# A two-block model on one core: the mixer in a new order, and norm passes and output products that wait tile by tile

## The chip, the cores and the metric

One core of one Trainium2 chip runs the whole program in one launch. The metric is device time in microseconds (us), the median of several executions. In the rows PE is TensorE, DVE VectorE, ACT ScalarE, POOL GpSimd, SP the queue that issues the DMAs.

## The reference, cut to what matters

272 tokens (16 meta tokens and 256) of width 1024, all float32. The first block is a mixer and a PEER layer, the second block two layers of feed-forward, attention, feed-forward. The change lies in the mixer and at the joints of the second block.

```python
u = rmsnorm(h, norm_mix_w)                       # 272 x 1024
z, xbc, dt_raw, conf_in = split(u @ w_in)        # 1024 | 2048 | 16 | 2048
xbc = silu(causal_depthwise_conv(xbc, 4 taps))   # -> xs, bm, cm
dt = softplus(dt_raw + dt_bias)
y = ssd_chunked(xs * dt, ...) + D * xs           # chunked scan over 16 + 128 + 128 tokens
y = groupnorm(y * silu(z)) * norm_w              # y_ssd, 1024 wide
a, g = split(conf_in)
c = causal_depthwise_conv(a * sigmoid(g), 31 taps)
c = silu(layernorm(c) * g + b)                   # y_conf, 1024 wide
h = h + concat(y_ssd, y_conf) @ w_out            # 2048 x 1024
# second block, four times:
h = h + 0.5 * swiglu(rms_norm(h), wi, wo)        # 1024 -> 2 x 2816 -> 1024
```

## The kernel before, in words

Activations lie transposed, features on the 128 partitions in 8 chunks k and tokens on the columns. Weights stream from HBM in units of 128 x 1024 (512 KB) through a ring of four slots. SP (`stream`, L414) reloads a slot once `unit_done` says that the unit before in that slot is used up.

A product of the projections is a *split* product (`split`, L484): ACT copies the unit rounded to fp32r (`part_high`, L388), POOL or DVE subtracts for the remainder (`part_low`, L394), and PE adds three products for each of 8 chunks (L489 to L491): 24 instructions for a unit. The activations are split the same way into `hw_hi` and `hw_lo` (`gain`, L1040). A few products use plain float32 (`whole`, L476; L480), 8 products for a unit, which the trace records as two instructions each.

The order of the work is written out by hand for each engine; engines meet only through counting semaphores, and an instruction that waits holds up all behind it on its engine.

**The mixer before.** The residual h is weighted by the norm's gain and split (L1087 to L1089); the division by the root mean square (`rstd`) is done on every result. PE sums the squares (`stats`, L497), projects dt in plain float32 (L559), and then runs 16 units of `conf`, 16 of `xbc`, 8 of `z` (L654 to L673). DVE goes through 36 events (L1225): it scales a result into SBUF (L1135, L1147 or L1231), does the 4-tap convolution of an xbc unit (L1151, L1153: source SBUF, sum in PSUM), and from event 4 on an eighth-size task of the 31-tap convolution, `conv_taps` (L1114; L1125: 248 taps on 128 x 256, in two alternating sums in PSUM). ACT and DVE run the softplus of dt (L1095 to L1112) before the first event. The scan has eight steps: `decay_rows` on PE, `decay_in` on DVE, `row_exp` on ACT, `decay_out` on DVE, a product with `ecs` on POOL (L2029), `mix_step` on PE, `keep_y` on DVE. Most of them run after the last tap. Then come the layer norm of the conformer half (`mean_mm`, `centred`, `var_mm`), the group norm of the scan half, and, when all 16 chunks of `mix` are ready (L695), the output product: `loop_pair` takes two units for each of 8 output chunks, and DVE adds each to h and splits it (`add_pair`, L1055). SP asks for the `query` weights only after the keys and the spill of h (L435 to L439).

**The joints of the second block.** A feed-forward (`ffn`, L777, L1446, L1863) is 44 units in and 24 units out. PE waits before the out part for all 22 chunks of `gated` (L782). Before the next norm it sums eight chunks of squares, eight plain float32 products (`stats`), and then waits for all eight chunks of `hw`.

Of the kernel before, what the change touches and what calls it, by code (L numbers as in the profile page):

```python
# [14 lines left out]
P = 128  # L15
D = 1024
KD = D // P
# [29 lines left out]
    ("conf", 16, 8, 16, 4), ("xbc", 16, 8, 16, 4), ("z", 8, 8, 8, 4),  # L47
    ("mix_out", 16, 8, 8, 2), ("query", 16, 8, 16, 4),
# [73 lines left out]
def build(nc, a, out):  # L122
    h_spill = nc.dram_tensor("h_spill", (P, KD, SEQ), F32, kind="Internal").ap()
    bias_rows = nc.dram_tensor("bias_rows", (HEADS, P * REL), F32, kind="Internal").ap()
    with ExitStack() as ctx:
# [80 lines left out]
        stat_ready, std_ready, rstd_ready = sem("stat_ready"), sem("std_ready"), sem("rstd_ready")  # L206
        dve_step = sem("dve_step")
# [19 lines left out]

        NORM = {n: i for i, n in enumerate(["mix", "peer", "final", "ffn1", "a", "ffn2", "ffn3", "b", "ffn4"])}
# [5 lines left out]

        with nc.sbuf_tensor("before", [P, GATED_AT], F32):
# [7 lines left out]
        pair_at = m1.at  # L243
        pair_a, pair_g = m1(2, T), m1(2, T)
        state_at = m1.at
        raw = m1(4, SSD_TAPS - 1 + T)
        conv = m1(4, T)
# [5 lines left out]
        hw_mix = m1(KD, T)  # L253
# [6 lines left out]
        b_tok = m1(2, GROUPS * P)  # L260
        ecs, dec_l = m1(2, 512), m1(2, 512)
        m1_end = m1.at
        m1.at = state_at
        state = m1(2, D)
        m1.at = pair_at
        cs_c = m1(2, 512)
        m1.at = pair_at
        gate_std = m1(GROUPS, SEQ)
        gate_rstd = gate_std
        xdtd = Carve(sq[:, :, :].rearrange("p k t -> p (k t)"), KD * T)(2, D)  # L270
        u_rows = big[0:HEADS, P * SEQ - REL:P * SEQ]
        assert m1_end <= P * SEQ - REL
# [57 lines left out]
        sig_ready = sem("sig_ready")  # L330
# [76 lines left out]
        def _(sp):  # L407
# [22 lines left out]
            for s in range(RING):  # L430
                load_unit("conf", s, s)
            stream("conf", 1)
            for name in ("xbc", "z", "mix_out"):
                stream(name)
            sp.wait_ge(hw_ready, 8 * NORM["peer"] + 8)  # L435
# [3 lines left out]
            stream("query")  # L439
# [32 lines left out]
        def _(pe):  # L472
# [11 lines left out]
            def split(units, b, bank_out, hi, lo, m=KD, k0=0, start=True, stop=True):  # L484
# [19 lines left out]

            def bank_wait(name, i, banks):

                o = OUT0[name] + i
                if o >= 4:
                    pe.wait_ge(acc_free, o - banks + 1 if i >= banks else o - 3 if name in ("xbc", "z") else OUT0[name])

            def straight(name, i, parts, n, banks=4):
# [1626 lines left out]
```

## Time and profile before

| | us |
|---|---|
| median of 3 runs (2571.82 to 2574.12) | 2573.2 |
| the profiled execution | 2573.35 |
| its span in the trace | 2571.6 |
| PE busy, share of the span | 2312.1 (90%) |
| DVE busy | 1701.1 (66%) |
| ACT busy | 1245.5 (48%) |
| POOL busy | 189.6 (7%) |

The span runs from the first to the last instruction; the profiled execution's own time is 1.75 us more, and lies 0.15 us above the median. The mixer takes the first 373 us, the rest of the first block lasts until about 1263 us, the second block until the end. Busy shares are averages over stages that have different limits.

### The profile page before, as it was taken

Reading aid. Unit: us, or ns where it says so; the run is one execution under the profiler, and the core shown is the slowest. Engines: PE = TensorE matmul, PEld = TensorE weight load, DVE = VectorE, ACT = ScalarE, POOL = GpSimd, SP = SyncE. Lnnn points to the kernel's source line nnn. Section 1 sums busy time; section 2 is a strip of 40 time slices with the busy share of each in tenths; the row PEclk is TensorE's granted clock in tenths of the full one; section 3 lists DMA queues with packets and bytes.
Section 4 is the critical chain, followed back from the end, with each engine's and each line's share of the span. In section 5 each row is a group of like instructions: output and inputs, shape, how many; then the busy total and the mean of one; then the engine's idle time right before and its main releaser. Section 6 shows DMA issues by size and latency. Waiting matters only on the chain.

```text
span 2571.6 us, 43283 instructions
## 1 busy us (share of the span) xinstructions
PE 2312.1 (90%) x15506; PEld 2110.3 (82%) x15506; DVE 1701.1 (66%) x3103; ACT 1245.5 (48%) x1699; POOL 189.6 (7%) x90
## 2 busy tenths in 40 slices
PE   6848679999997899999699996889999999869999
PEld 6747569999997788888599995569999997647999
DVE  6997427999957755555766557457656754854774
ACT  3323215777776655555466343426546632323653
POOL 4433000000005500000200000000000000000000
PEclk9988889999999999999899997589999999989999
DMA  4321745555552166666455552025565553202555
GB/s 141 123 74 58 115 141 164 185 183 187 184 184 66 38 189 189 189 188 188 139 173 176 169 169 66 0 87 175 163 184 168 171 173 106 66 17 68 186 171 180
DMA packets 107932, 359.35 MB, mean 140 GB/s; under 512 B 12976, under 2 KB 21552, under 8 KB 107728
## 3 DMA queue, kind: packets, MB, share of 16 engines
q1 hardware_dynamic: 105792, 354.04, 43.8%
q10 hardware_dynamic: 2064, 4.33, 1.5%
q8 instruction: 45, 0.74, 0.1%
q14 instruction: 31, 0.25, 0.0%
HBM read 351.90 MB, written 6.42 MB: 139 GB/s over the span
## 4 chain that ended last, share of the span: by engine, by line
PE 78%; DVE 16%; issue 3%; ACT 1%; DMA 1%; SPq 0%; POOL 0%; DVEq 0%; ACTq 0%; POOLq 0%
PE ps L489 17%; PE ps L491 17%; PE ps L490 17%; PE ps L752 14%; PE ps L480 5%; DVE ps L1125 3%; PE ps L502 1%; DVE hot_keys L1387 1%; DVE big L1488 1%; PE ps L981 1%; DVE ps L1153 1%; DVE big L1621 1%; DVE hw_hi L1043 1%; PE ps L920 1%; DVE big L1560 1%
## 5 line engine op out<-in xcount | busy, mean ns | idle before, releaser
L489 PE MATMUL ps<-hw_hi,w_hi 128*128 128x272 f32 (+1 forms) x3104 | 897.0, 289 | 63.4 <-POOL ring_lo L394 25.0
L388 ACT ACTIVATE w_hi<-ring 128x1024 fp32r<-128x1024 f32 x612 | 646.7, 1058 | 523.9 <-DMA ring<-in_ffn_in_dram 148.9
L491 PE MATMUL ps<-hw_hi,ring_lo 128*128 128x272 f32 (+1 forms) x3104 | 893.5, 288 | 0.0
L490 PE MATMUL ps<-hw_lo,w_hi 128*128 128x272 f32 (+1 forms) x3104 | 892.3, 287 | 0.0
L394 DVE TENSOR_TENSOR ring_lo<-ring,w_hi 128x1024 fp32r<-128x1024 f32 x572 | 698.5, 1221 | 215.8 <-ACT w_hi L388 211.5
L489 PEld LDWEIGHTS ps<-hw_hi,w_hi 128*128 128x128 f32 x3104 | 594.6, 192 | 68.9 <-issue 41.0
L491 PEld LDWEIGHTS ps<-hw_hi,ring_lo 128*128 128x128 f32 x3104 | 594.5, 192 | 0.0
L490 PEld LDWEIGHTS ps<-hw_lo,w_hi 128*128 128x128 f32 x3104 | 592.9, 191 | 0.3
L752 PE MATMUL ps<-w_hi,hid_parts 128*128 128x512 f32 x1024 | 280.7, 396 | 2.3 <-DVE hid_parts L1414 2.3
L752 PEld LDWEIGHTS ps<-w_hi,hid_parts 128*128 128x128 f32 x1024 | 193.5, 189 | 47.7 <-issue 2.5
L489 PE MATMUL ps<-gated_hi,w_hi 128*128 128x272 f32 (+1 forms) x704 | 205.2, 291 | 13.2 <-DVE gated_lo L1468 13.2
L491 PE MATMUL ps<-gated_hi,ring_lo 128*128 128x272 f32 (+1 forms) x704 | 204.4, 290 | 0.0
L490 PE MATMUL ps<-gated_lo,w_hi 128*128 128x272 f32 (+1 forms) x704 | 204.1, 290 | 0.0
L1455 DVE TENSOR_TENSOR big<-ps,rstd 128x272 f32<-128x272 f32 (+1 forms) x176 | 77.0, 438 | 135.0 <-PE ps L491 129.5
L752 PE MATMUL ps<-ring_lo,hid_parts 128*128 128x512 f32 x512 | 161.2, 396 | 0.0
L489 PEld LDWEIGHTS ps<-gated_hi,w_hi 128*128 128x128 f32 x704 | 135.9, 193 | 14.0 <-issue 14.0
L480 PE MATMUL ps<-big,ring 128*128 128x256 f32 (+1 forms) x512 | 118.3, 395 | 22.0 <-DVE big L1276 15.8
L490 PEld LDWEIGHTS ps<-gated_lo,w_hi 128*128 128x128 f32 x704 | 136.0, 193 | 0.0
L491 PEld LDWEIGHTS ps<-gated_hi,ring_lo 128*128 128x128 f32 x704 | 135.6, 193 | 0.0
L480 PEld LDWEIGHTS ps<-big,ring 128*128 128x128 f32 x512 | 100.5, 197 | 40.0 <-issue 16.2
L1825 ACT ACTIVATE hid_parts<-big 128x256 fp32r (+1 forms) x128 | 53.4, 418 | 133.4 <-PE ps L752 129.8
L752 PEld LDWEIGHTS ps<-ring_lo,hid_parts 128*128 128x128 f32 x512 | 96.9, 189 | 22.6
(343 smaller groups left out, 2536.0 us busy)
## 6 DMA issues: line engine op xcount, KB each, us to landing
ring<-in_ffn_in_dram SPq DMA_DIRECT2D x176, 512.0 KB, 3.4
ring<-in_down_dram SPq DMA_DIRECT2D x128, 512.0 KB, 3.4
ring<-in_up_dram SPq DMA_DIRECT2D x128, 512.0 KB, 3.4
ring<-in_ffn_out_dram SPq DMA_DIRECT2D x96, 512.0 KB, 3.5
ring<-in_a_in_dram SPq DMA_DIRECT2D x24, 512.0 KB, 3.5
ring<-in_conf_dram SPq DMA_DIRECT2D x16, 512.0 KB, 3.5
ring<-in_xbc_dram SPq DMA_DIRECT2D x16, 512.0 KB, 3.4
ring<-in_mix_out_dram SPq DMA_DIRECT2D x16, 512.0 KB, 3.4
```

Source lines behind the costliest of these rows:

```text
L388: nc.scalar.activation(w_hi[:, u % RING, :], ring[:, u % RING, :], ACT.Copy).then_inc(hi_done, 1)
L394: eng.tensor_tensor(ring_lo[:, u % RING, :], ring[:, u % RING, :], w_hi[:, u % RING, :].bitcast(F32), ALU.subtract).then_inc(split_done, 1)
L480: last = nc.tensor.matmul(bank_out, ring[:, s, k * P:(k + 1) * P], rhs(k0 + k), start=start and k == 0, stop=stop and k == KD - 1)
L489: nc.tensor.matmul(bank_out, w_hi[:, b, w], hi(k0 + k), start=start and k == 0, stop=False)
L490: nc.tensor.matmul(bank_out, w_hi[:, b, w], lo(k0 + k), start=False, stop=False)
L491: last = nc.tensor.matmul(bank_out, ring_lo[:, b, w], hi(k0 + k), start=False, stop=stop and k == m - 1)
L502: last = nc.tensor.matmul(ps[:, 4, c0:T], C(matrix), sq[:, k, c0:T], start=k == 0, stop=k == KD - 1)
L752: last = nc.tensor.matmul(ps[:, 2 * t + half, :], hid_parts[:, part, t * P:(t + 1) * P], weight[:, s, half * 512:(half + 1) * 512], start= ...
L920: last = nc.tensor.matmul(ps[:, (b + 2) % 4, 0:SEQ], ring[:, u % RING, c0:c0 + P], lat[:, k, META:T], start=k == 0, stop=k == 1)
L1125: relay(V_.scalar_tensor_tensor(sums[k % 2], x, V("conf_w", j * CONF_TAPS + k), sums[k % 2], ALU.mult, ALU.add), k == CONF_TAPS - 1)
L1455: V_.tensor_tensor((up_a, up_b)[s % 2][:, p, c0:T], ps[:, s, 0:T - c0], rstd[:, c0:T], ALU.mult).then_inc(acc_free, 1)
L1825: A_(hid_parts[:, c % PARTS, :], at(hid, it * 4 + c), ACT.Copy).then_inc(hid_hi_done, 1)
```

## The change

What it does, stage by stage:

- The mixer's residual is scaled by its norm's gain and by `rstd` first, and then split; results of xbc, conf and z need no scaling. The squares are added in pairs on DVE, so that four products and not eight make the mean. dt is projected as a split product after the second xbc unit.
- The order of units is xbc, conf, z. The 4-tap convolution reads PSUM and sums in SBUF. The softplus of dt lies between the first five xbc events.
- The 31-tap convolution is dealt out: 11 taps after every conf pair (88), 7 in every step of the scan (56), 16 after the gating of y, and the last 88 after the group norm.
- A scan step goes with every z unit. z is copied by ACT, and its silu is done after the last step.
- The output product runs in two halves of the contraction: eight units that need only the scan half, eight that need the conformer half, into the same eight half-banks. `add_halves` adds them to h in the second half.
- SP loads the first four query units ahead of the keys and the spill.
- In the second block, before a, ffn2, ffn3, b and ffn4, POOL adds the eight chunks of squares into one (`sum_squares`), PE makes one product of it, and does so after the first unit of the next stage. That unit waits for `hw` chunk by chunk. ffn1 keeps its old statistics. The out part of every feed-forward waits for `gated` in three portions.
- At the end of a feed-forward's out part DVE splits h before it makes the last unit's remainder; one rounding and one remainder of the next stage are moved ahead of the root and the reciprocal.

```diff
-    ("conf", 16, 8, 16, 4), ("xbc", 16, 8, 16, 4), ("z", 8, 8, 8, 4),
-    ("mix_out", 16, 8, 8, 2), ("query", 16, 8, 16, 4),
+    ("xbc", 16, 8, 0, 4), ("conf", 16, 8, 0, 3), ("z", 8, 8, 0, 3),
+    ("mix_out", 16, 8, 8, 4), ("query", 16, 8, 16, 4),
...
+            for i in range(UNITS["mix_out"]):
+                half, j = i // KD, i % KD
+                u = UNIT0["mix_out"] + i
+                sp.wait_ge(unit_done, u - RING + 1)
+                load_unit("mix_out", 2 * j + half, u % RING)
+            stream("query", 0, 1)
...
                 for k in range(m):
+                    if normed_before is not None:
+                        pe.wait_ge(hw_ready, normed_before + k + 1)
...
+            def summed_stats(norm, c0):
+                pe.wait_ge(sq_sum, (KD - 1) * (SUMMED[norm] + 1))
+                nc.tensor.matmul(ps[:, 4, c0:T], C("mean_d"), sq[:, 0, c0:T], start=True, stop=True).then_inc(stat_ready, 1)
...
+                        if s < 3:
+                            pe.wait_ge(gated_ready, g0 + min(KD * (s + 1), FF_CHUNKS))
...
+            for e in range(16):
+                if e >= 4:
+                    pe.wait_ge(xconv_ready, e - 3)
+                mixed("xbc", e, e % 4, T, normed(0), 0 if e == 0 else None)
+                if e == 1:
+                    project_dt()
+                if e == 9:
+                    turn_dt()
+                if e == 12:
+                    cumulate()
             for e in range(16):
+                if e < 3:
+                    pe.wait_ge(xconv_ready, 13 + e)
+                else:
+                    pe.wait_ge(glu_done, (e - 3) // 2 + 1)
+                mixed("conf", e, e % 3, T, normed(0))
+                if 2 <= e < 5:
+                    turn_chunk(e - 2)
+                if e in (8, 10):
+                    states((e - 8) // 2)
+            decay_rows(0)
             for e in range(KD):
+                if e < 3:
+                    pe.wait_ge(glu_done, (13 + e) // 2 + 1)
+                else:
+                    pe.wait_ge(z_raw, e - 2)
+                mixed("z", e, (16 + e) % 3, SEQ, normed(META))
+                if e < 7:
+                    decay_rows(e + 1)
+                mix_step(e)
...
+            def out_half(half, ready):
+                for j in range(KD):
+                    u = UNIT0["mix_out"] + KD * half + j
+                    pe.wait_ge(slot_loaded[u % RING], (u // RING + 1) * 16)
+                    if half and j >= 4:
+                        pe.wait_ge(acc_free, OUT0["mix_out"] + j - 3)
+                    for k in range(KD):
+                        if j == 0:
+                            pe.wait_ge(ready, k + 1)
+                        last = nc.tensor.matmul(ps[:, (0, 1, 2, 5)[j % 4], (j // 4) * SEQ:(j // 4 + 1) * SEQ],
+                                                ring[:, u % RING, k * P:(k + 1) * P], mix[:, KD * half + k, :],
+                                                start=half == 0 and j < 4 and k == 0, stop=half == 1 and k == KD - 1,
+                                                skip_group_check=True)
+                    last.then_inc(unit_done, 1)
...
+            def xbc_event(i):
+                x, acc = ps[:, i % 4, 0:T], conv[:, i % 4, :]
+                dve.wait_ge(unit_done, UNIT0["xbc"] + i + 1)
+                if i >= 4:
+                    dve.wait_ge(xbc_ready, i - 3)
+                link(V_.tensor_scalar(acc, x, V("ssd_w", i * 4 + 3), V("ssd_b", i), ALU.mult, ALU.add))
+                for k in (2, 1, 0):
+                    late = SSD_TAPS - 1 - k
+                    ins = V_.scalar_tensor_tensor(acc[:, late:T], x[:, 0:T - late], V("ssd_w", i * 4 + k), acc[:, late:T],
+                                                  ALU.mult, ALU.add)
...
+            for i in range(5, 16):
+                xbc_event(i)
+                if i == 10:
+                    copy_dt()
+                if i == 13:
+                    copy_cum()
+            for e in range(16):
+                if e % 2:
+                    gate_pair(e // 2)
+                if 3 <= e < 6:
+                    scale_x(e - 3)
+                if e in (9, 11):
+                    keep_state((e - 9) // 2)
+                if e % 2:
+                    conv_taps(11)
+            for i in range(8):
                 decay_in(i)
+                conv_taps(3)
+                if i >= 1:
+                    keep_y(i - 1)
                 decay_out(i)
+                conv_taps(4)
...
+            def sum_squares(norm, c0):
+                at0 = (KD - 1) * SUMMED[norm]
+                for k in range(1, KD):
+                    pool.wait_ge(sq_ready, 8 * NORM[norm] + k + 1)
+                    if k > 1:
+                        pool.wait_ge(sq_sum, at0 + k - 1)
+                    nc.gpsimd.tensor_tensor(sq[:, 0, c0:T], sq[:, 0, c0:T], sq[:, k, c0:T], ALU.add).then_inc(sq_sum, 1)
```

## Rows read from the trace of the kernel before

**Rows 1.** Stretches of the mixer; busy us of each engine, granted clock, DMA share, GB/s

```profile
40.00:218.00 178.00, 131.81 (x929) 126.19 (x927) 169.00 (x393) 53.05 (x73) 87.73 (x38) 0.88 0.34 107
...
218.00:295.00 77.00, 42.95 (x305) 37.17 (x306) 42.71 (x81) 28.00 (x51) 11.86 (x9) 0.82 0.51 70
...
295.00:354.00 59.00, 58.25 (x256) 50.45 (x256) 9.52 (x23) 0.00 (x0) 0.00 (x0) 0.95 0.42 117
...
354.00:374.00 20.00, 6.63 (x21) 5.47 (x22) 3.04 (x4) 6.23 (x13) 0.00 (x0) 0.57 0.59 210
```

**Rows 2.** Timeline of the start: start us, length us, instruction

```profile
12.51 6.36 PE L502 MATMUL ps<-sq,con 128*128 128x272 f32 x16
...
19.43 1.85 DVE L1037 RECIPROCAL rstd<-std 128x272 f32<-128x272 f32 x1 [2.85 <-ACT std L1702]
...
31.26 0.57 PE L489 MATMUL ps<-hw_hi,w_hi 128*128 128x272 f32 x1 [8.62 <-POOL ring_lo L394]
...
40.29 0.77 DVE L1135 TENSOR_TENSOR big<-ps,rstd 128x272 f32<-128x272 f32 x2
```

**Rows 3.** A stretch in which PE never waits, columns as in rows 1

```profile
1430.00:1480.00 50.00, 50.00 (x402) 50.00 (x401) 29.23 (x37) 21.80 (x25) 0.00 (x0) 1.00 0.62 190
```

**Rows 4.** Timeline of DVE, 106 to 114 us

```profile
106.96 0.44 DVE L1147 TENSOR_TENSOR big<-ps,rstd 128x272 f32<-128x272 f32 x1
...
109.53 0.43 DVE L1142 TENSOR_TENSOR big<-big 128x272 f32<-128x272 f32 x1
...
110.00 3.23 DVE L1125 SCALAR_TENSOR_TENSOR ps<-big,vec,ps 128x256 f32<-128x256 f32 x8
...
113.14 0.44 DVE L1147 TENSOR_TENSOR big<-ps,rstd 128x272 f32<-128x272 f32 x1
```

**Rows 5.** Timeline, 28 to 39 us: POOL beside DVE

```profile
28.68 9.90 POOL L394 TENSOR_TENSOR ring_lo<-ring,w_hi 128x1024 fp32r<-128x1024 f32 x4 [18.16 <-ACT w_hi L388]
...
31.30 2.49 DVE L1105 TENSOR_TENSOR big<-big 16x272 f32<-16x272 f32 x1
```

**Rows 6.** Groups of instructions in the mixer, 0 to 385 us: busy, mean ns, idle before

```profile
L388 ACT ACTIVATE w_hi<-ring 128x1024 fp32r<-128x1024 f32 x46 | 47.8, 1051 | 107.8 <-DMA ring<-in_query_dram 85.5 <-DMA ring<-in_conf_dram 22.3
...
L394 POOL TENSOR_TENSOR ring_lo<-ring,w_hi 128x1024 fp32r<-128x1024 f32 x40 | 95.6, 2397 | 102.0 <-ACT w_hi L388 102.0
```

**Rows 7.** Page, DMA issues: size and us to landing

```profile
ring<-in_xbc_dram SPq DMA_DIRECT2D x16, 512.0 KB, 3.4
```

**Rows 8.** Timeline of DVE in the scan: a step start

```profile
233.79 0.42 DVE L1245 TENSOR_TENSOR big<-ps,rstd 128x256 f32<-128x256 f32 x1 [7.74 <-PE ps L491]
...
248.89 0.69 DVE L1206 TENSOR_TENSOR big<-ps,big 128x512 f32<-128x512 f32 x1 [0.63 <-PE ps L632]
...
251.94 0.69 DVE L1206 TENSOR_TENSOR big<-ps,big 128x512 f32<-128x512 f32 x1 [0.24 <-PE ps L632]
```

**Rows 9.** Timeline of the output product and what follows

```profile
294.80 58.45 PE L480 MATMUL ps<-big,ring 128*128 128x256 f32 x256 [15.76 <-DVE big L1276]
...
373.23 0.47 PE L489 MATMUL ps<-hw_hi,w_hi 128*128 128x256 f32 x1
```

**Rows 10.** Waits of PE after 385 us: total, times, longest

```profile
PE ps L489 <- DVE gated_lo L1468: 13.2, 4, 3.3
```

**Rows 11.** Two stretches just after that wait, columns as in rows 1

```profile
1418.00:1424.00 6.00, 6.00 (x28) 6.00 (x29) 1.92 (x2) 1.06 (x1) 0.00 (x0) 0.52 0.02 4
...
1860.70:1864.00 3.30, 3.24 (x14) 3.25 (x15) 2.09 (x2) 1.06 (x1) 0.00 (x0) 0.50 0.02 5
```

**Rows 12.** Timeline at two norm passes after a residual add

```profile
1486.69 3.83 PE L502 MATMUL ps<-sq,con 128*128 128x272 f32 x16
...
1720.45 3.83 PE L502 MATMUL ps<-sq,con 128*128 128x272 f32 x16
...
1721.95 2.35 DVE L394 TENSOR_TENSOR ring_lo<-ring,w_hi 128x1024 fp32r<-128x1024 f32 x2
...
1723.92 0.49 PE L489 MATMUL ps<-hw_hi,w_hi 128*128 128x272 f32 x1
```

More of the change, by code:

```diff
@@ L226, in chain @@
             return link, relay
+        SUMMED = {n: i for i, n in enumerate(["a", "ffn2", "ffn3", "b", "ffn4"])}
         NORM = {n: i for i, n in enumerate(["mix", "peer", "final", "ffn1", "a", "ffn2", "ffn3", "b", "ffn4"])}
@@ L1075, in add_three @@
                         gain(base, j, c0)
+                    if final and base is not None:
+                        low(name, e + 2)
             def add_single(name, base, c0):
@@ L1268, in _ @@
-            link(V_.reciprocal(rstd[:, 0:SEQ], std[:, 0:SEQ]))
-            for k in range(KD):
-                V_.tensor_tensor(conf[:, k, :], conf[:, k, :], rstd[:, 0:SEQ], ALU.mult).then_inc(ln_in, 1)
+            conv_taps(16)
             for half in range(2):
@@ L1447, in ffn, with group @@
                 g0 = FF_CHUNKS * (f - 1)
-                invert(f"ffn{f}", c0)
                 name = f"ffn{f}_in"
                 u0 = UNIT0[name]
-                with dve.Fori(0, FF_CHUNKS // 2) as it:
+                if f > 1:
+                    low(name, 2)
+                invert(f"ffn{f}", c0)
+                def group(it, first):
                     for s in range(RING):
@@ L1456, in ffn @@
                                          ALU.mult).then_inc(acc_free, 1)
-                        low(name, s + 2, it)
+                        if not (first and s == 0):
+                            low(name, s + 2, it)
                         if s % 2:
@@ L1469, in ffn @@
                                              ALU.subtract).then_inc(gated_ready, 1)
+                if f > 1:
+                    group(0, True)
+                with dve.Fori(1 if f > 1 else 0, FF_CHUNKS // 2) as it:
+                    group(it, False)
                 add_three(f"ffn{f}_out", base, c0)
             ffn(1, 0, VEC["ln_mix"])
+            low("a_in", 2)
             invert("a", 0)
@@ L1734, in _ @@
+            for e in range(4, 18):
+                high("xbc", e)
+                if e >= 7:
+                    xbc_silu(e - 4)
+                if e == 15:
+                    act.wait_ge(cum_mm, 1)
+                    A_(cum[0:META, 0, HEADS:2 * HEADS], ps[0:META, 4, HEADS:2 * HEADS], ACT.Exp).then_inc(cum_exp, 1)
+                    A_(cum[:, 1, HEADS:3 * HEADS], ps[:, 4, 4 * HEADS:6 * HEADS], ACT.Exp).then_inc(cum_exp, 1)
+            xbc_silu(14)
+            xbc_silu(15)
             for e in range(16):
@@ L1872, in ffn @@
                             A_(up_a[:, p, c0:T], up_a[:, p, c0:T], ACT.Silu).then_inc(silu_ready, 1)
+                if f > 1:
+                    group(0, True)
+                with act.Fori(1 if f > 1 else 0, FF_CHUNKS // 2) as it:
+                    group(it, False)
                 name = f"ffn{f}_out"
@@ L2007, in _ @@
             nc.gpsimd.tensor_copy(ident_bf[:, :], ident).then_inc(pads_clear, 1)
[L2009 to L2010 removed]
+            for e in range(UNITS["xbc"] + 10):
+                part_low(nc.gpsimd, "xbc", 0, e)
             for c in range(2):
[L2012 to L2013 removed]
                 n = CHUNKS[c][1]
@@ L2049, in _ @@
             nc.gpsimd.tensor_tensor(bias[:, :, :], bias[:, :, :], bc(mask[:, 0, :], 1, HEADS), ALU.add).then_inc(bias_ready, 1)
+            def sum_squares(norm, c0):
[5 more added lines that the diff above has]
+                    nc.gpsimd.tensor_tensor(sq[:, 0, c0:T], sq[:, 0, c0:T], sq[:, k, c0:T], ALU.add).then_inc(sq_sum, 1)
+            for norm in ("a", "ffn2", "ffn3", "b"):
+                sum_squares(norm, 0)
+            sum_squares("ffn4", META)
 def column_blocks(w):
```

414 lines of the change are left out of this document (196 added, 218 removed).

## The prediction

> **What bounds the kernel now.** I read the page first: PE is busy for nine tenths of the span, but its tenths sag in the first 15%, where DVE shows 9 after 9. Then busy time by stretch, for the mixer alone [rows 1]. From 40 to 218 us DVE works 169.0 of 178 us and PE 131.8: the 31-tap convolution bounds this stretch. From 218 to 295 us nobody is full (PE 42.95, DVE 42.71 of 77): a chain of latencies, in which each engine waits for another. From 295 to 354 us PE works alone on the output product (DVE 9.5 of 59), and from 354 to 374 us PE is busy for 6.6 of 20. Third, the timeline of the start: the first product of a unit comes at 31.26 us and DVE takes the first result at 40.29 us [rows 2]. In the second block PE never waits inside a feed-forward: 402 products in 50 us, 0.124 us each [rows 3], so whatever PE no longer does or waits for there comes off the time one to one, unless something else is late.
>
> **The start.** Four mean products replace eight: 6.36 us for eight at the start [rows 2], so 3.2 us from 12.5 to 15.7 us. The root (1.1 us, an estimate with its table load) and the reciprocal (1.85 [rows 2]) give 18.7 us. New on this path are 8 scalings, 8 roundings on ACT that run beside them, and 8 subtractions. An operation of this kind takes 0.43 us with its wait and about 0.35 without [rows 4], so the first unit could start at 21.8 us. POOL is in the way. While it worked for 9.90 us on four remainders, a DVE operation of 0.43 us took 2.49 us and ended with one of them [rows 5]; I add 1.5 us of that: 23.3 us. The rule behind it is in the Trainium skill, "SBUF — State Buffer", section "Who interferes with whom": DVE with two SBUF inputs and a GpSimd operation that reads SBUF lock each other out. The trace agrees.
>
> The rule speaks against this change, since it puts POOL's remainders beside more such DVE work (scalings, softplus) and adds 35 POOL sums. Events read PSUM and are free of it: L1147 stays at 0.44 us beside POOL [rows 4]. Counting every lock-out gives 301 us for the end of the mixer below, counting none 293.
>
> **xbc.** A unit is 24 products, 3.0 us [rows 3]. The first runs cold, +1.5 us, and ends at 27.9 us. Three more and the dt product, also 24 instructions, end at 40 us. The fifth unit's rounding now stands on ACT behind the softplus and three silus, which wait for DVE's third event; ACT's 1.05 and POOL's 2.4 us for it follow [rows 6]. I put this stall at 6.3 us. Twelve units of 3.0 us, 1.5 us cold and 3 us of small products bring the end to 86.7 us. Does DVE keep up? An event cost 2.57 us, from 106.96 to 109.53 [rows 4], and loses its first instruction, about 0.5. What the trace lacks is a tap from PSUM into SBUF; bounds are 1.7 us for an event (every instruction at 0.43 us) and 2.6 (no gain); I take 2.0, which is 2.57 less that first instruction, since the three accumulating taps stay. Both ends stay under 3.0, so they move the sum by 2 us at most. The weights keep up too: 3.4 [rows 7] + 1.05 + 2.4 us [rows 6] in a ring of four units of 3.0 us.
>
> **conf.** Sixteen units, 48 us; transposes and states about 9 us beside no cover; alternation between PE and DVE 6 us: 149.5 us. DVE's share is less: 88 taps at 0.39 us (3.14 us for eight [rows 4]) make 35 us, with gates, scalings and states 48.
>
> **z and the scan.** Before, a step with no tap in it took 3.05 us and a step with a z unit 11 us, 7.74 of it waiting for PE [rows 8]. In the new step 7 taps (2.75 us), three operations of the scan of 0.69 us [rows 8], their waits and `keep_y` (0.6) make 6.0 us of DVE work. PE needs 2.8 + 1.3 + 1.0 us, inside it. Eight steps: 198 us. The chain of latencies of before now lies under taps.
>
> **To the last tap.** Gating 2.8, 16 taps 6.3, a wait of 2.6 for the statistics, group norm 10 (four reciprocals of 1.8 [rows 2] and eight scalings): 220 us. Then 88 taps, 34.5, and three closings of 1 us: 258 us. The first half of the output product, 8 units of 3.65 (58.45 us for 16 [rows 9]), 29 us, starts at about 212 us and is free, as long as these taps cover it; bare it would cost 29 us.
>
> **The tail.** Mean product 0.5, eight subtractions 2.8, a square and its product 1.2, root 1.8, reciprocal 1.85, first scaling and silu 1: 268 us with the waits. Second half of the product, 29.2 us: 297 us. The query weights are there, so only eight mean products of 0.43 us stand before the first query product: 301 us. Before it came at 373.23 us [rows 9]. **Mixer: -72 us.** The keys and the spill, 1 MB each, now lie beside the loading of query unit 5, which has over 8 us of slack.
>
> **Joints of the feed-forwards.** The wait for the last `gated` is 13.2 us in four [rows 10]. After it PE runs at half clock: granted 0.52 over 6 us, a loss of 2.9 us, and 0.50 over 3.3 us, a loss of 1.65 [rows 11]; the others I take at 1.65. With 8 chunks needed for the first unit and all 22 only 6 us later, both go: -21 us. Before a, ffn3 and b, eight statistics products (3.83 us [rows 12]) become one: -3.0 each, -9, because the first unit's weights and chunks are ready. POOL's last sum (about 0.65 us, from 2.4 for 1024 columns [rows 6]) ends as the first unit does. Before ffn2 and ffn4 the statistics were a cover: product 1 came at 1723.92, and the first remainder of two of 1.2 us from 1721.95 on would allow 1723.15 [rows 12]. This saves 0.8, costs one product of 0.45, and uncovers an idle gap of 2.7 us, after which the clock should fall as it did after 3.3 us: +1.5 each, +3.
>
> **Sum.** -72 - 21 - 9 + 3 = -99 us against the profiled execution's 2573.35: 2474 us. That execution lies 0.15 us above the median of the runs shown, so the median moves alike.
>
> **Rival 1, a larger gain.** DVE is never kept waiting and nothing is locked out. Its work from 28 us on is 16 events (31), softplus and copies (13), 248 taps with closings (106), gates, scalings and states (12), scan (22), norms (13): 197 us, so the last tap falls at 225 instead of 258. That gives 2441 us. For it: DVE had only 9 idle us in 178 before [rows 1]. Against it: xbc now has no taps beside it, and DVE must idle while PE makes 3.0 us units.
>
> **Rival 2, a smaller gain.** The scan steps stay ruled by PE's round trips. If a step costs 9 us instead of 6, because PE falls idle in each and takes its z unit at half clock (5.3 us), the stage is 24 us longer: 2498 us. For it: steps with a z unit took 11 us and PE's mean clock in the scan was 0.82 [rows 1, 8]. Against it: `decay_rows` is now issued a step ahead.
>
> **Rival 3, slower.** One mechanism: the short waits between units, one in nearly each of 40, keep PE at 1.2 GHz through the whole mixer. Each of 40 units costs 2.6 us more (granted 0.52 [rows 11]), 104 us, of which DVE's work could hide some; the eight bare units of the product double, +28. If all of it showed, 2474 + 104 + 28 = 2606 us. It decides from the point where the 99 us are eaten, three quarters of this. Against it: with the waits of before the clock from 40 to 218 us was still 0.88 [rows 1].
>
> **Rival 4, it doesn't do what it says.** The dealt-out taps are a fixed list; if the last 88 ended before the first half of the product did, that half would be bare and the fall 15 to 20 us smaller. Here taps end at 258 and the half at 242, so the margin is 16 us.
>
> **Numbers.** My forecast with its neighbours (2460 to 2488) 0.58; rival 1 0.14; rival 2 0.20; rival 4 0.05; rival 3 0.02; other 0.01. The range leaves out the far half of rival 1 and what lies beyond rival 2: 2450 to 2502. A measurement of this kernel can tell 0.2%, 5 us, from no change; only rival 3 reaches it. Faster 0.97, same 0.01, slower 0.02.
>
> **What would show it.** First unit product near 23 us; a stall of some 6 us before the fifth unit; xbc done near 87, conf near 150, z near 198 us; last tap near 258 us; first query product near 301 us. No wait of PE for the last `gated`, and full clock behind it; one statistics product after the first unit of a, ffn2, ffn3, b, ffn4, and a low clock only in ffn2 and ffn4. I am wrong if the first query product comes outside 285 to 325 us, if more than half of the first output half is waited for, or if the second block shortens by less than 18 or more than 35 us.

## The result, and the profile after

The changed kernel takes 2490.64 us (median of 4 runs, 2487.36 to 2492.97) against 2572.51 of the kernel before in the same runs: ratio 0.9682, 95% interval 0.9665 to 0.9699. The forecast was 2474 us with a range of 2450 to 2502. So the sign and the range held, but 99 us were forecast and 82 came. The profiled execution took 2490.17 us, with a span of 2488.3: 83.2 us less than the one of before.

The page of the changed kernel: busy time, and PE's tenths over the granted clock, in 40 slices of 62 us.

```profile
span 2488.3 us, 42956 instructions
...
PE 2286.5 (92%) x15436; PEld 2086.0 (84%) x15436; DVE 1697.3 (68%) x3067; ACT 1169.0 (47%) x1652; POOL 228.8 (9%) x124
...
PE   6987999999978999999699988799999998778999
...
PEclk8997999999999999999899996599999999989999
```

Busy time by stretch of the mixer, the same view as [rows 1]: conf, the scan, the tail with the first output half, and the second half.

```profile
93.00:152.00 59.00, 54.15 (x402) 51.98 (x401) 45.07 (x103) 19.90 (x26) 39.80 (x18) 0.97 0.42 130
152.00:200.00 48.00, 42.08 (x388) 39.24 (x387) 47.49 (x110) 19.29 (x33) 24.25 (x14) 0.96 0.29 90
200.00:260.00 60.00, 44.02 (x155) 35.10 (x156) 58.06 (x134) 7.59 (x19) 0.00 (x0) 0.77 0.82 145
260.00:302.00 42.00, 37.43 (x165) 32.08 (x164) 18.82 (x43) 14.51 (x29) 0.00 (x0) 0.96 0.35 108
```

Before, nobody was full from 218 to 295 us; now PE is busy for 54 of the 59 us of conf, and DVE for all but 2 us of the scan and of the tail. The timeline of PE and DVE at the places that the prediction named (these rows answer to [rows 2, 8, 9]):

```profile
22.34 0.56 PE L506 MATMUL ps<-hw_hi,w_hi 128*128 128x272 f32 x1 [5.85 <-DVE hw_lo L1156]
...
45.92 0.57 PE L506 MATMUL ps<-hw_hi,w_hi 128*128 128x272 f32 x1 [6.06 <-POOL ring_lo L403]
...
93.91 0.44 DVE L1227 TENSOR_TENSOR big<-ps,big 128x272 f32<-128x272 f32 x1 [4.32 <-ACT big L1819]
...
199.94 0.61 DVE L1290 SCALAR_TENSOR_TENSOR big<-big,vec,ps 128x128 f32<-128x128 f32 x2
...
213.04 2.04 PE L732 MATMUL ps<-big,ring 128*128 128x256 f32 x4 [3.72 <-DVE big L1329]
...
242.05 15.87 PE L732 MATMUL ps<-big,ring 128*128 128x256 f32 x64 [7.65 <-DMA ring<-in_mix_out_dram]
...
261.48 2.74 DVE L1335 TENSOR_TENSOR big<-big,ps 128x256 f32<-128x256 f32 x8 [2.86 <-PE ps L742]
...
302.28 0.47 PE L506 MATMUL ps<-hw_hi,w_hi 128*128 128x256 f32 x1
```

The first query product comes at 302.28 us where it came at 373.23. The second block, at the joint of ffn2 (this answers to [rows 10, 11]; the second line is a stretch behind it), and in front of ffn2's first unit, where the prediction expected its only loss. First all waits of PE for the last eviction at a joint, then the stretch, then timeline and stretch at the norm pass:

```profile
PE ps L506 <- DVE big L1520: 3.6, 4, 0.9
```

```profile
1784.90:1790.00 5.10, 4.98 (x40) 4.98 (x41) 4.19 (x6) 1.97 (x2) 0.00 (x0) 1.00 0.49 124
```

```profile
1643.10 7.82 POOL L2154 TENSOR_TENSOR sq<-sq 128x272 f32<-128x272 f32 x7 [228.03 <-ACT sq L1771]
...
1646.02 0.88 DVE L1097 SCALAR_TENSOR_TENSOR hw_lo<-h,vec,hw_hi 128x272 fp32r<-128x272 f32 x1
1646.82 5.18 DVE L403 TENSOR_TENSOR ring_lo<-ring,w_hi 128x1024 fp32r<-128x1024 f32 x3
...
1648.85 0.57 PE L506 MATMUL ps<-hw_hi,w_hi 128*128 128x272 f32 x1 [3.75 <-DVE ring_lo L403]
...
1653.35 0.62 PE L525 MATMUL ps<-sq,con 128*128 128x272 f32 x2
```

```profile
2286.80:2291.80 5.00, 0.90 (x5) 0.90 (x5) 4.87 (x5) 2.69 (x4) 4.28 (x6) 0.85 0.39 105
2291.80:2296.80 5.00, 5.00 (x25) 4.91 (x24) 2.22 (x2) 0.00 (x0) 1.13 (x1) 0.50 0.00 0
```

At the joint 0.9 us are left of 3.3 and the clock behind it is 1.00. At the norm pass POOL's seven sums stand together, 1.12 us each; beside them DVE's remainders cost 1.73 us each (5.18 for three), and the gain's second part 0.88 instead of 0.50. PE waits 3.75 us, and 4.1 in front of ffn4, where it then runs at a granted 0.50.

### The profile page after: what moved, and what is told of

Read it like the earlier page. It is cut to its first block, busy times and chain, and to the rows that moved or that the text cites. A ratio compares the mean times of both kernels' runs of the same rounds, so it can differ in the third digit from the quotient of the medians.

```text
span 2488.3 us, 42956 instructions
## 1 busy us (share of the span) xinstructions
PE 2286.5 (92%) x15436; PEld 2086.0 (84%) x15436; DVE 1697.3 (68%) x3067; ACT 1169.0 (47%) x1652; POOL 228.8 (9%) x124
## 4 chain that ended last, share of the span: by engine, by line
PE 81%; DVE 13%; issue 2%; DMA 2%; ACT 1%; POOL 0%; DVEq 0%; SPq 0%; ACTq 0%
PE ps L506 18%; PE ps L508 18%; PE ps L507 18%; PE ps L804 14%; PE ps L495 2%; PE ps L732 2%; DVE hot_keys L1449 1%; DVE ps L1214 1%; DVE big L1561 1%; PE ps L1034 1%; DMA ring<-in_mix_out_dram 1%; DVE hw_hi L1096 1%; DVE big L1695 1%; DVE big L1633 1%; PE ps L973 1%
## 5 line engine op out<-in xcount | busy, mean ns | idle before, releaser
L2154 POOL TENSOR_TENSOR sq<-sq 128x272 f32<-128x272 f32 (+1 forms) x35 | 38.8, 1107 | 1047.5 <-ACT sq L1973 587.4
L2133 POOL TENSOR_TENSOR diff<-con,slot_t 128x1024 f32<-128x1024 f32 x32 | 64.6, 2023 | 547.0 <-DVE slot_t L1427 526.4
```

What stands on the lines that cost most here:

```text
L2133: nc.gpsimd.tensor_tensor(diff[:, b, :, :], bc(C("iota"), 1, 8), bc(keys, 2, P), ALU.subtract).then_inc(hot_diff, 1)
L2154: nc.gpsimd.tensor_tensor(sq[:, 0, c0:T], sq[:, 0, c0:T], sq[:, k, c0:T], ALU.add).then_inc(sq_sum, 1)
```

## Where the 83 us come from

I compare the places at which PE stops in both traces. The shift of each such place, and what it grew by since the one before:

| place | before | after | shift | step |
|---|---|---|---|---|
| first query product | 373.2 | 302.3 | -70.9 | mixer -70.9 |
| transposes of the routing | 791.7 | 722.8 | -68.9 | query +2.0 |
| end of ffn1's in units | 1414.6 | 1345.8 | -68.8 | 0 |
| a's head statistics | 1546.3 | 1470.8 | -75.5 | ffn1 joint -4.8, norm a -1.9 |
| end of ffn2's in units | 1857.4 | 1784.1 | -73.3 | norm ffn2 +2.2 |
| end of ffn3's in units | 2065.4 | 1985.8 | -79.6 | ffn2 joint, norm ffn3 -6.3 |
| b's index logits | 2175.1 | 2089.1 | -86.0 | ffn3 joint, norm b -6.4 |
| b's wait for the selection | 2258.1 | 2173.3 | -84.7 | +1.3, no edit in it |
| b's transposes behind the selection | 2279.0 | 2195.4 | -83.6 | +1.2, no edit in it |
| end of ffn4's in units | 2498.8 | 2419.5 | -79.4 | norm ffn4 +4.2 |
| last product | 2566.1 | 2482.8 | -83.3 | ffn4 joint -3.9 |

So the mixer was 1 us off, the query 2 and the second block 13 (-14.4 against -27). The two steps in b are changes of the clock and not of the work (behind the selection it was granted 0.73 over 6 us before and 0.54 after): in the traces of the kernels below, which have b's code unchanged, the first of the two stretches took 81.3 to 84.3 us (83.0 before, 84.3 in the changed kernel) and the second 5.1 to 6.5 (5.1 before, 6.2 in the changed kernel). Likewise ffn4's in part with its norm took 132.6 us in the changed kernel's trace and 131.0 to 131.1 in six of the eight others with the same code there (132.0 and 132.6 in the other two), so up to 1.6 us of its +4.2 are chance.

The experiments go after the terms of the second block first, then after what bounds the new mixer. Of the mixer's 71 us only the hidden half of the output product is tested by taking it out; that the rest comes from the scaled activations, the taps dealt out and the scan beside z is read from the traces and shown by no run.

## The experiments

All are edits of the changed kernel, so their ratios stand against its 0.9682. A ratio's interval is about 0.0015 to either side, 4 us, and a difference of two of them some 5 us; where the effect is smaller, the verdict rests on the stage of the trace that the edit touches.

### POOL's sums: pe_sums_2 and pe_sums_5

```
 def summed_stats(norm, c0):
+    if norm not in SUMMED: return stats(norm, c0)
-SUMMED = {... "a", "ffn2", "ffn3", "b", "ffn4"}
+SUMMED = {... "a", "ffn3", "b"}     (pe_sums_2)
+SUMMED = {}                         (pe_sums_5)
```

> The changed kernel, with the squares of ffn2 and ffn4 no longer summed on POOL: PE does eight statistics products there, still behind unit 0 and with the tile-wise waits kept. Theory (the seven POOL sums of 1.1 us each lock DVE's last gains and lows: lows of 1.7 us where 1.22 would do, gaps of 3.75 and 4.10 us before unit 0 where 2.7 was forecast, and a lower clock after the gap): lows back at 1.22 us, both gaps at 2.4 to 3.0 us, fourteen more products on PE (+1.6 us), together 3 us faster than the changed kernel (1 to 6), 2487.6 us. Rival 1 (the gap is the chain h addition, gain, unit 0 by itself and POOL has no part in it): gaps unchanged, 1.6 us slower. Rival 2 (POOL's sums hide at no cost and the lower clock decides): within 1 us of the changed kernel.

> As pe_sums_2, but the statistics of all five norms go back to eight products on PE behind unit 0. Theory (in front of a, ffn3 and b the squares come one every 9 us, POOL's sums are spread out and lock nothing that is waited for): seven more products at each of the three, 0.8 us each, so 2.4 us slower than pe_sums_2 and about 0.6 us faster than the changed kernel, 2490 us. Rival (POOL's sums cost DVE something there too): no slower than pe_sums_2.

pe_sums_2: ratio 0.9693 [0.9679, 0.9706], 2.8 us slower, which the medians alone can't tell from no change. pe_sums_5: 0.9726 [0.9713, 0.9740], 8.5 us slower again. Both expectations are wrong in the same term. The timeline of pe_sums_2 in front of ffn2, PE and DVE:

```profile
1646.89 0.36 PE L506 MATMUL ps<-hw_hi,w_hi 128*128 128x272 f32 x1 [2.81 <-DVE ring_lo L403]
1651.50 3.83 PE L519 MATMUL ps<-sq,con 128*128 128x272 f32 x16
```

```profile
1645.00 0.50 DVE L1099 SCALAR_TENSOR_TENSOR hw_lo<-h,vec,hw_hi 128x272 fp32r<-128x272 f32 x1
1645.42 3.49 DVE L403 TENSOR_TENSOR ring_lo<-ring,w_hi 128x1024 fp32r<-128x1024 f32 x3
```

Eight statistics products take 3.83 us, one takes 0.62: a norm costs 3.2 us more with eight, not 0.8. I had priced them like unit products of 0.12 us, against the prediction's own [rows 12]. With that, pe_sums_2 adds 6.4 us of products and is 2.8 us longer in the two stages (ffn2 2.38, ffn4 0.45), so POOL's sums cost 3.6 us there; against the 131.0 us that most other traces show for ffn4 it's 2 us. The gap fell from 3.75 and 4.10 to 2.81 and 2.79 and the remainders from 1.73 to 1.16 us each, as the theory had it. pe_sums_5 adds 3 x 3.2 = 9.6 us and is 8.5 longer: in front of a, ffn3 and b the sums on POOL hide nearly whole. So by the trace's stages POOL's sums pay everywhere, and least where they stand close together.

### The joints: joint_whole and joint_free

```
 def loop_3(name, parts, n, g0):
+    pe.wait_ge(gated_ready, g0 + FF_CHUNKS)     (joint_whole)
-    pe.wait_ge(acc_free, o0)                    (joint_free)
...
-            if s < 3:
-                pe.wait_ge(gated_ready, ...)    (joint_whole)
```

> The changed kernel, with the old wait at the joint of the four FFNs: all 22 tiles gated before the first out unit. Theory (of the 17 us that the joints gained 9.6 are the shorter gaps, 0.91 us in place of 3.30, and the rest is the clock that no longer falls behind the gap): gaps back at 3.3 us, a cold stretch behind each, 17 us slower, 2507.6 us (15 to 20). Rival (the clock would stay up, or it fell for another reason): 9.6 us slower, 2500 us.

> The changed kernel, without the wait for the last in unit's eviction in front of the out loop, as the waits on the single banks cover it. Theory (the 0.91 us gap that is left at each joint is that eviction alone): the four gaps go to under 0.2 us, 3 us faster, 2487.6 us (2 to 4). Rival (behind it stands another wait, for the lows of the first out unit or for the last two gated tiles): the gap moves into the third out unit or stays, under 1 us faster.

joint_whole: 0.9742 [0.9729, 0.9755], 15.4 us slower; in the trace the four stages from the last in unit to the last out unit are 18.3 us longer. joint_free: 0.9659 [0.9643, 0.9675], 5.9 us faster. Waits of PE in joint_whole, and the stretches behind its four joints:

```profile
PE ps L506 <- DVE gated_lo L1533: 13.2, 4, 3.3
```

```profile
1352.30:1358.00 5.70, 5.68 (x25) 5.69 (x26) 2.04 (x2) 1.06 (x1) 0.00 (x0) 0.51 0.00 0
1795.70:1801.00 5.30, 5.29 (x23) 5.30 (x24) 2.04 (x2) 1.06 (x1) 0.00 (x0) 0.50 0.02 5
2002.40:2008.00 5.60, 5.56 (x32) 5.57 (x33) 2.07 (x2) 1.06 (x1) 0.00 (x0) 0.70 0.01 3
2436.40:2442.00 5.60, 5.60 (x35) 5.60 (x36) 1.99 (x2) 1.06 (x1) 0.00 (x0) 0.70 0.01 3
```

The 13.2 us of [rows 10] are back to the tenth. Of the 15.4 us (18.3 in the trace), 9.6 are gaps and the other 6 to 9 products at a low clock, granted 0.50 to 0.70: the joint's term is shown, both halves of it. What the prediction missed is the 0.9 us that stays at each joint: the loop's own first line waits until all evictions of the in units are done. joint_free takes that line out, and the trace then has no gap at any joint. The four stages are 4.6 us shorter, 3.6 of it the gaps; what the medians show beyond that is within what two measurements differ by.

### In front of ffn2 and ffn4: ffn_order

```
 ACT:  for k in range(KD):
+          if 5 <= k < 7: high(then, k - 5)
           square(k)
-      high("ffn2_in", 0), high("ffn2_in", 1)   in front of the squares
 DVE:  for j in range(KD):
           add, gain(j)
+          if 5 <= j < 7: low(then, j - 5)
-      first_lows("ffn2_in")                    (ffn4_in alike)
```

> The changed kernel, with ACT's squares of the first five tiles in front of the roundings of the first two ffn2 and ffn4 units, and DVE's low parts of these two units behind the gains of tiles 5 and 6. Theory (unit 0 waits 3.75 and 4.10 us because DVE does the low part behind the last gain, and because POOL's seven sums stand close together and lock it; neither has to be there): gaps under 1 us, POOL's sums one every 3.7 us, the clock stays up behind them, 8 us faster (5 to 11), 2482 us. Rival (the products of unit 1 and the eviction of unit 0 wait for the statistics instead, so most of it comes back as a wait for rstd within the first group): 3 us faster or less.

0.9624 [0.9607, 0.9642], 14.9 us faster by the medians; by the two stages of the trace 4.6 and 6.4, 11 us, of which up to 1.6 us are the chance in the changed kernel's ffn4. The medians' figure holds more chance. PE, POOL and the stretches in front of ffn2 and ffn4:

```profile
1646.97 0.40 PE L506 MATMUL ps<-hw_hi,w_hi 128*128 128x272 f32 x1 [0.53 <-DVE h L1136]
1650.11 0.62 PE L525 MATMUL ps<-sq,con 128*128 128x272 f32 x2
```

```profile
1636.46 1.01 POOL L2152 TENSOR_TENSOR sq<-sq 128x272 f32<-128x272 f32 x1 [2.65 <-ACT sq L1773]
1640.61 1.66 POOL L2152 TENSOR_TENSOR sq<-sq 128x272 f32<-128x272 f32 x1 [3.14 <-ACT sq L1773]
```

```profile
1647.00:1652.00 5.00, 5.00 (x38) 4.92 (x39) 2.76 (x4) 2.55 (x4) 1.02 (x1) 1.00 0.41 112
...
2285.00:2290.00 5.00, 5.00 (x44) 4.97 (x43) 3.12 (x4) 3.68 (x5) 0.00 (x0) 1.00 0.48 130
```

The gap is 0.53 us, the granted clock stays at 1.00 in these stretches, and POOL's sums come one in 3.7 us: 1.01 us with DVE silent, 1.66 beside a DVE remainder. The rival (the wait comes back for the statistics) fell. The loss that the prediction had booked as unavoidable was an order of instructions on ACT and DVE, which the change had left as it was.

### The output product's first half: half_bare_2, spread_z, taps_14_2, spread_taps

half_bare_2 moves the call:

```
-out_half(0, y_norm)
 ... mean product, variance product ...
+out_half(0, y_norm)
 out_half(1, mix_ready)
```

> The changed kernel, with the first half of the output product moved behind the product of the variances, right in front of the second half. Theory (the first half costs 29 us and lies whole beside DVE's last taps, its wait of 7.65 us for a transfer too): it starts where PE now waits for the normed tiles, about 264 us, and ends at 293 instead of the second half's start at 269.7, so 24 us slower, with up to 6 us more for a clock that is low at its start: 2515 us (2511 to 2520). Rival (the first half only displaces waits that would otherwise be there, or DVE's taps ran slower beside it): under 15 us slower.

0.9764 [0.9745, 0.9782], 21.1 us slower (21.4 by the first query product of the trace). The half is hidden, as the theory had it, and DVE's taps ran no faster without it: from PE's sums for the group norm to the end of the last closing it's 55.5 us in both traces. Moved, it cost the low end of what I expected: the two halves run from 265.15 us on as one group of 256 instructions in 55.4 us, without the 7.65 us wait and over what was PE's wait for the normed tiles.

```
-conv_taps(11)
+conv_taps(14)
```

> The changed kernel, with 14 taps of the causal convolution behind each conf pair instead of 11. Theory (DVE idles 14 us of the 59 us of the conf units, and is full from there on, so 24 taps of 0.47 us moved forward leave the tail shorter by what fits the idle time): DVE busy 45 us to 55 us in that stretch, 7 us faster (3 to 11), 2482 us. Rival (PE is busy 54 of these 59 us and waits for the gates: taps in front of a gate push the conf units back by as much as the tail gains): within 1.5 us of the changed kernel.

0.9690 [0.9674, 0.9707], 2.1 us slower, which can't be told from no change: the rival. In the trace the last conf gate comes 3.4 us later (154.55 against 151.16), the scan starts 4.6 us later, and the first output half 4.1 us later. But then DVE finishes its taps early and waits:

```profile
266.22 2.73 DVE L1335 TENSOR_TENSOR big<-big,ps 128x256 f32<-128x256 f32 x8 [12.89 <-PE ps L742]
```

So with the taps moved forward the tail is not bound by taps: PE stands in the first output half until 262.7 us. In the changed kernel this wait is 2.86 us, and half and taps end together (257.9 and 258.6 us). The DMA view of the changed kernel, 195 to 245 us, shows what else holds the half up:

```profile
bias_rows<-big ACTq DMA_DIRECT2D x1, 4224.0 KB, 45.6
ring<-in_mix_out_dram SPq DMA_DIRECT2D x5, 512.0 KB, 15.4
```

ACT issues the bias rows' transfer behind the silus of z, and a weight unit takes 15.4 us beside it (the median of five; the four issued while it ran took 13.2 to 19.2) instead of 3.5.

```
+act.dma_start(bias_rows ...)      in front of the scan's loop
 for e in range(8): high("z", e + 2), row_exp(e), z_copy(e)
-act.dma_start(bias_rows ...)      behind the silus of z
```

> The changed kernel, with the transfer of the relative bias rows (4.2 MB, 45.6 us to landing, begun at 199 us behind the silus of z) issued before the z units, at about 157 us. Theory (this transfer takes the queues while the first output half wants a unit every 3.7 us: the units land in 15.4 instead of 3.5 us, PE waits 7.65 us, and the first half ends at 257.8 us, level with the last taps at 257.7; the z units, one every 5.4 us, can stand the same delay): the 7.65 us wait is gone, the first half ends near 248 us, the taps then set the end alone, DVE's wait for the mean falls from 2.86 to about 1 us, 2 us faster (1 to 3). Rival (the z units' loads come late and stretch the scan): slower.

> As spread_z, with 14 taps behind each conf pair besides, as in taps_14_2. Theory (there DVE ended its taps 12.9 us before the mean was there, since PE was held in the first output half by that transfer): with the transfer out of the way the centring starts at about 254 us instead of 261.5 (changed kernel) and 266.2 (taps_14_2), 7 us faster than the changed kernel (5 to 9), 2483 us. Rival (PE's first half is late because its own start depends on the scan, which comes 5 us later there): under 3 us faster.

spread_z: 0.9743 [0.9726, 0.9760], 15.7 us slower. spread_taps: 0.9703 [0.9686, 0.9721], 5.4 us slower. Half of the theory held: in spread_z PE has no wait for a transfer in the first half any more and DVE waits 1.38 us for the mean, not 2.86. The other half, that z can stand the delay, fell. Timeline of DVE in spread_z:

```profile
174.47 0.69 DVE L1283 TENSOR_TENSOR big<-big,ps 128x512 f32<-128x512 f32 x1 [5.34 <-ACT big L1847]
...
200.42 0.69 DVE L1283 TENSOR_TENSOR big<-big,ps 128x512 f32<-128x512 f32 x1 [7.63 <-ACT big L1847]
```

ACT rounds the next z unit ahead of the row exponentials, so a late transfer (a median of 13.4 us here, by its DMA view) stops ACT, and with it the scan: 5.3 and 7.6 us in two steps. In spread_taps it's 2.5 and 7.7 us. But spread_taps is 10.3 us faster than spread_z (5.2 us by the start of the second half): once no transfer holds the first half up, the taps moved forward do shorten the tail. I had checked only the slack of the ring, not what is queued behind the waiting instruction.

### The start, and the query: highs_first_2, query_load_2

```
+high("xbc", 4)                    (highs_first_2)
 act.wait_ge(dt_abs, 1)
...
+high("xbc", 5)
 act.wait_ge(dt_u, 1)
```

> The changed kernel, with ACT rounding the weights of x/B/C unit 4 before it waits for dt and those of unit 5 before the logarithm, instead of behind the softplus and three silus. Theory (the stall of 6.06 us in front of the fifth unit is ACT's order alone, and everything behind it is shifted whole since DVE is full from 152 us to the end of the mixer): fifth unit at 40 instead of 45.9 us, 4 us faster (3 to 6), 2486 us. Rival (the stall moves to unit 6 or 7, whose roundings still stand behind the softplus and the silus): under 2 us faster.

0.9672 [0.9656, 0.9688], 2.6 us faster, not to be told from nothing. The 6.06 us wait became three:

```profile
47.17 0.37 PE L506 MATMUL ps<-hw_hi,w_hi 128*128 128x272 f32 x1 [1.02 <-POOL ring_lo L403]
54.53 0.39 PE L506 MATMUL ps<-hw_hi,w_hi 128*128 128x272 f32 x1 [1.06 <-DVE big L1170]
60.94 0.39 PE L506 MATMUL ps<-hw_hi,w_hi 128*128 128x272 f32 x1 [3.13 <-DVE big L1170]
```

The stall moved, as the rival said, 5.2 us of it, and its releaser is now DVE's event; the second output half starts at 270.1 us, in the changed kernel at 269.7, so the mixer gained nothing. ACT's order was only the first of two causes. DVE's timeline shows the second:

```profile
44.75 2.56 DVE L1187 TENSOR_TENSOR big<-big 16x272 f32<-16x272 f32 x1
...
49.76 2.52 DVE L1190 TENSOR_TENSOR big<-big 16x272 f32<-16x272 f32 x1
52.32 0.56 DVE L1167 TENSOR_SCALAR big<-ps,vec 128x272 f32<-128x272 f32 x1
```

The event of unit 4 (52.32 us) stands behind the softplus steps, and three of these take 7.5 us beside POOL's remainders, where steps of their kind take 0.3 to 0.4 without POOL. A fourth (2.40 instead of 0.35) delays the event of unit 5, and the 3.13 us wait ends with that event. Which of the two counts more, the order on DVE or the lock-out, no run tests.

```
-stream("query", 0, 1)
+stream("query", 0, 2)             (units 0 to 7 first)
 keys
+stream("query", 2, 3)
 spill
-stream("query", 1)
+stream("query", 3)
```

> The changed kernel, with the keys' transfer behind query unit 8's and the spill's behind unit 12's, instead of both (2 MB) in front of unit 4's. Theory (unit 4's 512 KB took 7.6 us instead of 3.5 beside these 2 MB, which is the 1.7 us gap on PE at 314 us): the gap is gone, 1.8 us faster (1 to 2.5), 2488 us. Rival (the stall moves to the units behind the two transfers, or PE waits for the keys later): within 0.7 us of the changed kernel.

0.9662 [0.9647, 0.9677], 5.1 us faster; 2.0 us of that lie between the tail and the routing's transposes, and what is over can't be told from chance. The 1.73 us gap at 314 us is gone and no other came. In the changed kernel the transfer for query unit 4 is issued at 305.6 us, when the ring's slot is free, and lands after 313 us beside keys and spill: not late in issue but slow in passing.

### All together: all_five

Five edits: ffn_order, joint_free, query_load, the bias rows in eight pieces, and the taps dealt out by DVE's idle time ahead of each next gate.

```
-conv_taps(11)
+conv_taps((17, 19, 11, 16, 14, 11, 13, 11)[e // 2])
+spread(0..3)    ahead of scan steps 0, 2, 4, 6
+spread(4)       behind the silus of z
+spread(5..7)    behind output units 2, 4, 6
```

> Five edits of the changed kernel together. Outside the mixer: ffn_order (measured 11 us in its trace), joint_free (3 us in gaps, 6 us in its median) and query_load (2 us) should add up, 17 to 20 us. In the mixer: the bias rows' transfer in eight pieces of 0.53 MB, four within the scan at every other step (one step is 5.4 us, one piece about 5.7 us by 45.6 us for the whole), the others behind the silus of z and during the first output half; and the 24 more taps dealt out behind the conf pairs by the time DVE idled ahead of the next gate (17, 19, 11, 16, 14, 11, 13, 11). Theory (spread_z showed that the z units stand no delay of 13 us each, and that without that transfer PE has no transfer to wait for in the first half; taps_14_2 that 14 taps each push the gates back where DVE didn't idle): last gate of conf at 151 us as in the changed kernel, scan steps of 5.4 us, first half without a stall of over 1 us and ended at 250 us, centring at 254 instead of 261.5 us, 7 us faster. Together 2464 us (2458 to 2471). Rival (the pieces still come too close together, and weights for z land late: idle time on ACT's row exponentials in the scan): mixer no faster or slower, 2471 to 2480 us.

2465.87 us (2464.38 to 2466.86), 0.9589 [0.9576, 0.9602]: 24 us faster than the changed kernel. Outside the mixer 21 us, as the parts add up to. In the mixer 3 us instead of 7. The pieces themselves do what they should:

```profile
ring<-in_mix_out_dram SPq DMA_DIRECT2D x11, 512.0 KB, 4.9
bias_rows<-big ACTq DMA_DIRECT2D x8, 528.0 KB, 7.2
ring<-in_z_dram SPq DMA_DIRECT2D x6, 512.0 KB, 5.9
```

There is no wait of PE for a transfer, and DVE idles nowhere in the scan. But the conf units came out later. PE, then DVE:

```profile
112.81 1.92 PE L624 MATMUL ps<-con,big 128*128 128x128 f32 x8 [5.12 <-DVE big L1253]
```

```profile
111.98 1.28 DVE L1253 TENSOR_TENSOR big<-ps,big 128x512 f32<-128x512 f32 x2
...
118.96 0.44 DVE L1229 TENSOR_TENSOR big<-ps,big 128x272 f32<-128x272 f32 x1 [5.70 <-ACT big L1821]
...
258.70 2.74 DVE L1337 TENSOR_TENSOR big<-big,ps 128x256 f32<-128x256 f32 x8 [2.73 <-PE ps L742]
```

The gate stood at 113.09 us. PE waits 5.12 us ahead of it, at the transposes of the last chunk, for DVE's scaling of the chunk before, and that scaling is queued behind the 19 taps. The idle time ahead of a gate was not free: DVE's other work in the pair is waited for as well. The run moves taps and transfer at once, so it doesn't say what either is worth alone, and what the best deal of the taps is, stays open.

## Why the prediction was right, and where it was not

**The start.** First unit product 22.34 us (23.3 forecast), stall before the fifth unit 6.06 (6.3), last event of xbc at 87.4 (xbc done 86.7). An event that goes from PSUM to SBUF costs 2.1 us, taken as 2.0. The 1.5 us of lock-out added ahead of the first unit didn't come: POOL's first two remainders ended at 18.4 us, before the eight scalings began at 18.9, and these took 0.35 us each. It came later: three of DVE's softplus steps beside POOL took 2.15 to 2.48 us instead of 0.3 to 0.4, as [rows 5] had shown, and PE waited for none of them here. The prediction's 293 and 301 us for no lock-out and every lock-out don't follow from its sum, which holds 1.5 us of it and gives 299.5 without.

**conf and z.** conf's last gate at 151.2 us (149.5); the scan's last `keep_y` at 199.9 (198). A step is 5.4 us, not 6.0, but the taps behind conf's last gate ran to 156 us first, so two errors cancelled. Rival 2 (9 us a step) is out, rival 3 (PE at 1.2 GHz) too: granted clock 0.97, 0.96 and 0.77 by stage. Rival 1 is out: in conf DVE waited 16.9 us for ACT's sigmoids, which stand behind PE's units. That a step went from the chain of latencies to 5.4 us of DVE's work is read from the trace; no run separates it from the rest of the mixer.

**The tail.** Last tap at 257.7 (258), second half at 269.7 (268), first query product at 302.3 (301). Mixer -70.9 against -72. Yet its claim of a margin, rival 4's 16 us, was wrong: the first half ended at 257.9, not 242. It left out the 7.65 us wait beside the bias rows, a low clock (0.77 in this stage: 35.8 us of products instead of 29.2), and 1.5 us of waits for the normed chunks of y, which DVE delivers two in 2.6 us; it also started 1 us later. That is the 16 us. That the time came out right is luck: the delays, in no term of the sum, used up the margin and only some 1.5 us more (DVE waits 2.86 us for the mean, and 1.38 in spread_z, where the half isn't held up).

**The query.** "Slack of over 8 us" for query unit 5 (unit 4, counted from 0) was a step that failed: its transfer took 7.6 us instead of 3.5 beside 2 MB, and 1.7 us came through, so its slack was some 2.4 us (an estimate from these three numbers). query_load_2 shows it.

**The joints.** -17 us against -21 (joint_whole gives back 15.4, give or take 5, and 18.3 in the trace). Missed: 0.9 us at each of four, for a wait in the loop's own first line. joint_free, without it, is 4.6 us shorter there, and with that the term comes to the forecast's -21.

**Norms a, ffn3, b.** -1.9, -2.4 and -2.4 against -3.0 each. The saving itself is as forecast: the eight products in front of ffn3 held PE for 3.3 us, and the one behind the first unit holds it for 0.4. Missed was that the first unit now waits 0.53 us for the last residual add, and in a a later unit 0.50 us more for its remainder.

**Norms ffn2 and ffn4.** +6.4 us against +3 (+2.2 and +4.2, the latter with up to 1.6 us of chance), a step that failed. POOL's sum was taken as 0.65 us, in proportion to a remainder's 2.4 us for 1024 columns. It takes 1.01 us alone and 1.12 in a row, so seven run for 7.8 us and lock DVE out of the remainders that unit 0 waits for. The gap was 3.75 and 4.10 us instead of 2.7, and the granted clock 0.83 and 0.67 over the ten microseconds that begin with it. Worse than the size: the loss was taken as unavoidable, and ffn_order shows that it was the order on ACT and DVE. The rule cited from the Trainium skill ("SBUF — State Buffer", "Who interferes with whom") was right here (a remainder 1.73 us beside the sums, 1.16 without), and I named these 35 sums as a case of it, but gave their lock-out no price outside the mixer.

**The second block** shortened by 14.4 us. I had written that I would be wrong below 18, and here I was. The three terms erred in the same direction (joints 4.4, norms a, ffn3 and b 2.3, norms ffn2 and ffn4 3.4), and b, with no edit in it, came out 2.5 us longer. The range covered them only because the mixer's rivals had made it wide, not by bounds of their own.

## What to carry to other kernels

A wait taken out by an order written by hand leaves the next one in the list: read, at each place that the change touches, the loop's first line and the instruction queued behind a wait, for both showed up here as a microsecond or more each. Spread helper work (sums on POOL, a long transfer) over the time in which its inputs come, instead of starting it when all are there; ffn_order changed nothing but the order and was the largest gain of a single edit. And idle time in a busy-time table is not slack: in taps_14_2 and all_five work moved into it came back as somebody else's wait, and so did the transfer that spread_z moved beside the z units.

## What the runs showed of the hardware

POOL's addition of two SBUF tiles of 128x272 took 1.01 us and its subtraction of two of 128x1024 2.4 us, so its time was not in proportion to the columns. Beside the additions DVE's remainder of 1.16 to 1.23 us became 1.73, and beside a remainder on POOL not only DVE's operations with two tiles in SBUF took 2.1 to 2.6 us, but also a `TENSOR_SCALAR` with one (L1189: 2.35, of a kind that takes 0.3 alone). The clock's answer to the same gap varies: behind the four equal waits of 3.3 us in joint_whole it was granted 0.51, 0.50, 0.70 and 0.70, and in b, where the code is the same, a stretch ran at a mean of 0.88 in the changed kernel (84.3 us) and 0.92 in ffn_order (81.7 us). The bias rows' transfer moved 4.3 MB in 2060 packets at 100 GB/s with the DMA engines' share at full, and the four weight units issued while it ran took 13.2 to 19.2 us instead of 3.5; in eight pieces (all_five) the units' medians were 4.9 and 5.9 us.
